# Tiles rounded up to 128 bytes, and root mean square norms rooted by ScalarE from the bank of sums

## The chip, the cores and the metric

The kernel runs on one core of a Trainium2 chip. The metric is the device time of one execution in microseconds (us). A core has five engines that run their own instruction streams and wait for each other by semaphores: PE (TensorE, matmuls; its weight loads are shown as PEld), DVE (VectorE), ACT (ScalarE), POOL (GpSimd) and SP (SyncE, which here issues the weight transfers). Matmuls write banks of PSUM, [128, 512] float32 each; everything else lives in SBUF, 128 partitions wide.

## What is computed

Two transformer-like blocks in a row over 512 tokens of width 1024, all float32. Cut to what matters here:

```python
def rms_norm(x, g):
    y = x * lax.rsqrt(jnp.mean(x * x, axis=-1, keepdims=True) + EPS)    # EPS = 1e-6
    return y * g

# first block
h = rms_norm(x, norm1_g) * (1 + sc1) + sh1
proj = h @ w_in + b_in                      # attention, and a convolution of three taps
y = concat([rms_norm(y_attn, ..), rms_norm(y_conv, ..)])
x = x + g1 * (y @ w_o)
h = rms_norm(x, norm2_g) * (1 + sc2) + sh2
u = h @ w_up                                # gate, val: 2 x 2816 columns
f = silu(causal_dwconv3(gate, w, b)) * val
x = x + g2 * (f @ w_down)
x = rms_norm(x, final_norm_g)
# second block, two layers: rwkv time mix, then a gated spatial unit, each with
# x = x + rms_norm(mixer(rms_norm(x)));  x = x + rms_norm(swiglu(rms_norm(x)))
```

The time mix shifts the tokens by one, `xx = shift(h) - h`, and projects `h + xx * mix` by three matrices of 1024 x 1024.

## The kernel before

Activations are kept transposed: a tile has 128 channels as partitions and the 512 tokens as its row, so x is [128, 8, 512]. The program is one straight line per engine (with loops over pairs of units inside the feed-forward stages), written out by hand, and the stages follow each other: setup, first mixer, first feed-forward stage (`ffn0`, with the convolution), both norms between the blocks, time mix (shift, 24 projection units, eight rounds of the block recurrence, output projection `out_tm`), second feed-forward stage (`ffn1`), gate stage (16 units, then output projection `out_gu`), third feed-forward stage (`ffn2`), output.

**Weight units.** Every large product goes by units of weights. SP loads a unit into `raw` (four slots), ACT copies its upper half as float32r into `whi` (line 226), DVE subtracts for the lower half `wlo` (line 232), and PE does three matmuls for each k tile (lines 247 to 249):

```python
pe.matmul(dst, hi, rhs_hi(k), start=first and k == 0, stop=False)
pe.matmul(dst, hi, rhs_lo(k), start=False, stop=False)
mm = pe.matmul(dst, lo, rhs_hi(k), start=False, stop=last and k == kts - 1)
```

A unit of eight k tiles is 24 matmuls of 128 x 128 weights with a moving tile of 512 columns in float32r. The moving tiles are fh_hi and fh_lo in the up parts of the feed-forward stages (44 units each), f_hi and f_lo in the down parts, xs_hi and xs_lo in the three projections of the time mix (24 units), h, ys, gh and us elsewhere. ACT may overwrite a half of `whi` when the unit two before is done; SP may overwrite `raw` when DVE has made the lower half.

**Norms.** There are twelve. ACT squares the tiles, POOL adds the squares (or PE sums tile by tile), and PE sums over the channels with a matrix of ones into bank 4 (`pe_sums`, lines 328 to 340, or `pe_sum_of`). Then DVE makes mean plus epsilon into the tile var (`dve_mean`, lines 344 and 446), ACT takes the root in place (`act_root`, line 326), and DVE the reciprocal (`dve_rstd`, line 351), after which the tile rstd is ready. The next sum into bank 4 waits for the semaphore of the mean (`var_ready`). The norms: norm1 (setup), norm_cv and norm_at (the two halves of the first mixer's output, right behind each other on the same bank), the norm before ffn0 (its tiles wait for rstd), norm_f (line 1573 takes the reciprocal of a second root made from another bank at the same time, `both`), the norms of the four outputs out_tm, ffn1, out_gu, ffn2 (their tiles are added to x only with rstd), and the norms led into ffn1, the gate stage (norm_g) and ffn2, whose rstd is applied only after the first products.

**Where tiles lie.** Tiles are placed one after another in each partition, every one at the next multiple of 32 bytes, and a later stage uses the bytes of an earlier one again. x, raw, whi, wlo, tmp, sq, var, rstd and vecs start at multiples of 128, and the first tile of a stage as well. Then, in bytes past a multiple of 128:

| tile ahead, its bytes | tiles behind it | before |
|---|---|---|
| gbuf [P, 2, 514], 4112 | fh_hi0, fh_lo0, gsq | 32 |
| hb [P, 8, 513], 16416 | xx, xs_hi, xs_lo | 32 |
| invf [P, 1], 4 | pos_i, spread, k_t, v_tok, prj, p_t | 96 |
| st [P, 2, 12], 96 | gb_sb, cbuf | 64 |
| cbuf [P, 2, 514], 4112 | cacc, ada_acc, x_tok, vrow, late | 96 |
| ends 96, nk_sb 32, ng_sb 32 | cent2 | 32 |
| cent2 [P, 64] 256, not_ka 32 | AR, B_t and all tiles of the block rounds | 64 |
| v_st [P, 56], 224 | v_tk, ws_in, wsT, bs_row, bs | 96 |

All other moving tiles of float32r products (h, f, ys, gh, us, and fh of the second and third feed-forward stages) are at 0.

Other lines that the prediction names: 938, 1020, 2542, 2936 (small float32 matmuls on k_t, p_t, cent2 and wsT), 648 (PE's first use of the constants that POOL makes at the start, which waits for 18 of them), 865 and 2072 (ACT from a bank with a bias column), 1510 and 1673 (DVE, lower halves of f and xs).

Of the kernel before, what the change touches and what calls it, by code (L numbers as in the profile page):

```python
# [22 lines left out]
ALU = mybir.AluOpType  # L23
# [14 lines left out]
KA = DA // P  # L38
RAW = 4
EPS = 1e-6  # L40
TWO_PI = 2 * np.pi
# [77 lines left out]
def build(nc, A, out):  # L119
# [25 lines left out]
    gain = sb("gain", [P, KD])  # L145
    cact = sb("cact", [P, KD])
    bank = [ctx.enter_context(nc.psum_tensor(f"bank{i}", [P, T], F32)) for i in range(8)]
    NORM_BANK, ADA_BANKS = 4, (7, 6, 6)
# [125 lines left out]
    class Norm:  # L274
# [4 lines left out]
        def __init__(self, src, n, ready, eps=EPS, rstd_=None, var_=None, slots=None):  # L279
            self.src, self.n, self.ready, self.eps, self.slots = src, n, ready, eps, slots  # L280
            self.rstd = rstd[:, :] if rstd_ is None else rstd_
            self.var = var[:, :] if var_ is None else var_
            self.sq0, self.acc0 = sq_ready.claim(n), acc_step.claim(0 if slots else n - 2)
            self.sum0, self.var0, self.std0, self.rstd0 = (
                c.claim(1) for c in (sum_step, var_ready, std_ready, rstd_ready))

# [37 lines left out]
        def act_root(self, act):  # L324
            act.wait_ge(var_ready.sem, self.var0 + 1)
            act.activation(self.var, self.var, ACT.Sqrt).then_inc(std_ready.sem, 1)

        def pe_sums(self, pe):
            wait(pe, var_ready.sem, self.var0)
            if self.slots is not None:  # L330
                for k in range(self.n):
                    pe.wait_ge(sq_ready.sem, self.sq0 + k + 1)
                    mm = pe.matmul(bank[NORM_BANK][:, :], ones[:, :], self.slots[k], start=k == 0, stop=k == self.n - 1)
                mm.then_inc(sum_step.sem, 1)
                return
            pe.wait_ge(acc_step.sem, self.acc0 + self.n - 2)
            pe.matmul(bank[NORM_BANK][:, :], ones[:, :], sq_sum[:, :], start=True, stop=False)
            pe.wait_ge(sq_ready.sem, self.sq0 + self.n)
            pe.matmul(bank[NORM_BANK][:, :], ones[:, :], sq[:, (self.n - 1) % 2, :], start=False, stop=True)\
              .then_inc(sum_step.sem, 1)  # L340

        def dve_mean(self, dve):
            dve.wait_ge(sum_step.sem, self.sum0 + 1)
            dve.tensor_scalar(self.var, bank[NORM_BANK][:, :], 1.0 / (self.n * P), self.eps,
                              ALU.mult, ALU.add).then_inc(var_ready.sem, 1)

        def dve_rstd(self, dve, mean=True):
            if mean:
                self.dve_mean(dve)
            dve.wait_ge(std_ready.sem, self.std0 + 1)  # L350
            dve.reciprocal(self.rstd, self.var).then_inc(rstd_ready.sem, 1)  # L351
            dve.wait_ge(rstd_ready.sem, self.rstd0 + 1)
# [69 lines left out]
    class LeadNorm(Norm):  # L422
# [3 lines left out]
        def __init__(self, src, n, ready):  # L426
            self.src, self.n, self.ready, self.eps = src, n, ready, EPS
            self.rstd, self.var = rstd[:, :], var[:, :]
            self.sq0, self.summed0 = sq_ready.claim(n), sq_summed.claim(n)
            self.var0, self.std0, self.rstd0 = (c.claim(1) for c in (var_ready, std_ready, rstd_ready))  # L430

# [5 lines left out]
        def pe_sum_of(self, pe, k):  # L437
            if k == 0:
                wait(pe, var_ready.sem, self.var0)
            pe.wait_ge(sq_ready.sem, self.sq0 + k + 1)  # L440
            pe.matmul(bank[NORM_BANK][:, :], ones[:, :], sq[:, k % 2, :], start=k == 0, stop=k == self.n - 1)\  # L441
              .then_inc(sq_summed.sem, 1)

        def dve_mean(self, dve):
            dve.wait_ge(sq_summed.sem, self.summed0 + self.n)
            dve.tensor_scalar(self.var, bank[NORM_BANK][:, :], 1.0 / (self.n * P), self.eps,
                              ALU.mult, ALU.add).then_inc(var_ready.sem, 1)

# [101 lines left out]
    c_row = sbs(mixer1, "c_row", [KD, P])  # L550
    invf = sbs(mixer1, "invf", [P, 1])
    pos_i = sbs(mixer1, "pos_i", [NT, P], I32)
    pos_f = sbs(mixer1, "pos_f", [NT, P])
# [5 lines left out]
    p_t = sbs(mixer1, "p_t", [P, 2, 4 * P])  # L559
    st = sbs(mixer1, "st", [P, 2, 12])  # L560
    gb_sb = sbs(mixer1, "gb_sb", [P, 2, T])
    cbuf = sbs(mixer1, "cbuf", [P, 2, T + 2])
    cacc = sbs(mixer1, "cacc", [P, 2, T])
# [39 lines left out]
    def pool_setup(pool):  # L603
# [31 lines left out]
        for q in range(NT):  # L635
            pool.wait_ge(const_ready, 14 + q)
            pool.affine_select(out=copies, in_=copies, compare_op=ALU.not_equal, fill=1.0, base=-32 * q,
                               pattern=[[0, NT], [-1, 32]], channel_multiplier=1).then_inc(const_ready, 1)

    CONSTS, MORE_CONSTS = 10, 18  # L640

# [496 lines left out]
    def dve_mixer1(dve):  # L1138
        dve_positions(dve)
        for n in range(len(BY_DVE)):  # L1140
            if n == 2:
                dve_angles(dve)
            if n == len(BY_DVE) - 4:
                norm1.dve_mean(dve)
            if n == len(BY_DVE) - 3:
                norm1.dve_rstd(dve, mean=False)
            dve_early(dve, n)
# [23 lines left out]
        norm_cv.dve_rstd(dve)  # L1171
        norm_at.dve_mean(dve)
        split_lo(dve, first[N_IN + 2])
        norm_at.dve_rstd(dve, mean=False)
        ada_add(dve, 1)
# [90 lines left out]
    class FFN:  # L1266
# [3 lines left out]
        def __init__(self, tag, at0, before, gains, shift, w_gate, w_up, w_down, conv, out_gains, final=False):  # L1270
# [7 lines left out]
            if conv:  # L1278
                self.gbuf = sbs(mem, "gbuf", [P, 2, T + 2])
            with ExitStack() as part:  # L1280
# [278 lines left out]
    def dve_both_norms(dve):  # L1559
# [10 lines left out]
           .then_inc(both_step, 1)  # L1570
        norm_f.dve_mean(dve)
        dve.wait_ge(both_std, 1)
# [8 lines left out]
    def dve_final(dve, k):  # L1581
        if k == 0:
            norm_f.dve_rstd(dve, mean=False)
        dve.scalar_tensor_tensor(x[:, k, :], x[:, k, :], v("final", k), rstd[:, :], ALU.mult, ALU.mult)\
# [18 lines left out]
    shift_mem = ExitStack()  # L1603
    hb = sbs(shift_mem, "hb", [P, KD, T + 1])
    xx = sbs(shift_mem, "xx", [P, KD, T])
# [219 lines left out]
    ng_sb = sbs(bm, "ng_sb", [P, 2 * NT])  # L1825
    cent2 = sbs(bm, "cent2", [P, CH])
    not_ka = sbs(bm, "not_ka", [P, KD])
# [613 lines left out]
    def dve_consts(dve):  # L2441
        dve.wait_ge(masks_ready, MASKS)
        dve.tensor_scalar(not_ka[:, :], vecs[:, col["k_a"]:col["k_a"] + KD], -1.0, 1.0, ALU.mult, ALU.add)\
           .then_inc(consts_ready, 1)
        dve.tensor_scalar(cent2[:, :], eye2[:, :], 1.0 / HD, None, ALU.subtract).then_inc(consts_ready, 1)

# [87 lines left out]
    def pe_turn_v(pe, n, j):  # L2534
# [5 lines left out]
        for t in range(NT):  # L2540
            for e in range(2):
                mm = pe.matmul(bank[Y_BANK[e]][:, col64(t)], v_[hr[e], t * P:(t + 1) * P], cent2[hr[e], :],  # L2542
                               start=True, stop=True)
# [327 lines left out]
    us_l = sbs(gu, "us_l", [P, KD, T], F32R)  # L2871
    v_st = sbs(gu, "v_st", [P, 6 * NT + NT * KD])
    v_tk = sbs(gu, "v_tk", [P, NT, D])
    ws_in = sbs(gu, "ws_in", [P, KD, P])
    wsT = sbs(gu, "wsT", [P, KD, P])
    bs_row = sbs(gu, "bs_row", [1, KD * P])
    bs = sbs(gu, "bs", [P, KD, P])
    LN_EPS = 1e-5
    gs_landed, wsT_done, wsT_ready, bs_done, bs_ready = (sem(n) for n in (
# [166 lines left out]
    def dve_gate(dve):  # L3046
# [58 lines left out]
        for n in range(N_GU):  # L3105
# [22 lines left out]
            if n == 0:  # L3128
                norm_g.dve_mean(dve)
                split_lo(dve, at_g(1).plus(2))  # L3130
                norm_g.dve_rstd(dve, mean=False)
            if n < N_GU - 1:
# [153 lines left out]
```

## Time and profile before

| | us |
|---|---|
| median of 3 runs | 2136.16 |
| lowest and highest run | 2132.23, 2136.9 |
| the profiled execution, its own time | 2140.12 |
| its span, first to last instruction | 2138.0 |

| engine | busy us | share of the span |
|---|---|---|
| PE | 1995.3 | 93% |
| DVE | 1080.3 | 51% |
| ACT | 781.2 | 37% |
| POOL | 240.9 | 11% |

The mean granted clock of PE is 0.957 of full. Times in the profile count from the start of the span. A matmul's busy time overlaps the next one's, so the pace of a stream is read from starts, not from durations. In a timeline a bracket at the end of a row is the idle time of the engine before it and who ended it; `x4` means four instructions merged in one row. A float32 matmul (not float32r) is shown as two passes.

### The profile page before, as it was taken

How to read it: one execution, taken by the hardware profiler on the slowest of the kernel's cores; microseconds unless marked ns; L12 is line 12 of the kernel's file. 1: busy time of each engine (PE TensorE's matmuls, PEld its weight loads, DVE VectorE, ACT ScalarE, POOL GpSimd, SP SyncE). 2: the span in 40 equal slices, each digit the busy share in tenths (PEclk: the TensorE clock that was granted, in tenths of full speed). 3: DMA queues.
4: the chain of work that ended last, by engine and by line, in shares of the span. 5: the costliest groups of instructions: out<-in, count | busy, mean ns of one | idle time of the engine just before them, and what ended most of it. 6: DMA issues, size and time to landing. Idle time of an engine off the chain costs nothing.

```text
span 2138.0 us, 35027 instructions
## 1 busy us (share of the span) xinstructions
PE 1995.3 (93%) x14351; PEld 1567.9 (73%) x14351; DVE 1080.3 (51%) x1579; ACT 781.2 (37%) x1237; POOL 240.9 (11%) x269
## 2 busy tenths in 40 slices
PE   6998989999997999899979899999979989999997
PEld 5776768888883677777757588888857858888885
DVE  6776765454325644678642644342265554443223
ACT  4333333333222345567523433322245443333221
POOL 1100000000024000322211011110100001111110
PEclk8999989999998999899988999999999989999998
DMA  9544223333332132000002133333222213333321
GB/s 299 173 123 128 79 68 89 98 88 113 95 90 59 59 90 73 6 10 10 5 26 69 51 97 98 98 113 103 80 57 82 79 53 98 95 98 105 109 81 40
DMA packets 311052, 181.02 MB, mean 85 GB/s; under 512 B 16381, under 2 KB 303763, under 8 KB 310932
## 3 DMA queue, kind: packets, MB, share of 16 engines
q1 hardware_dynamic: 305506, 162.29, 25.8%
q0 software_dynamic: 4608, 16.78, 2.5%
q8 instruction: 92, 1.51, 0.3%
q10 hardware_dynamic: 818, 0.21, 0.0%
q14 instruction: 28, 0.23, 0.0%
HBM read 177.16 MB, written 2.10 MB: 84 GB/s over the span
## 4 chain that ended last, share of the span: by engine, by line
PE 60%; DVE 5%; issue 5%; ACT 2%; POOL 1%; DVEq 0%; ACTq 0%; POOLq 0%
PE bank L247 16%; PE bank L249 15%; PE bank L248 15%; PE bank L1985 4%; PE bank L441 1%; PE bank L1775 1%; PE bank L2482 1%; PE bank L2476 1%; DVE rstd L351 1%; PE bank L2583 1%; POOL gsq L1449 1%; PE bank L2693 0%; PE bank L2542 0%; PE bank L2694 0%; DVE x L1240 0%
## 5 line engine op out<-in xcount | busy, mean ns | idle before, releaser
L232 DVE TENSOR_TENSOR wlo<-raw,whi 128x1024 fp32r<-128x1024 f32 (+1 forms) x262 | 340.6, 1300 | 711.7 <-ACT whi L226 711.7
L226 ACT ACTIVATE whi<-raw 128x1024 fp32r<-128x1024 f32 (+1 forms) x262 | 292.9, 1118 | 744.0 <-PE bank L249 736.6
L247 PE MATMUL bank<-fh_hi,whi 128*128 128x512 f32 x1056 | 420.4, 398 | 24.9 <-DVE fh_lo L415 17.4
L248 PE MATMUL bank<-fh_lo,whi 128*128 128x512 f32 x1056 | 414.7, 393 | 0.0
L249 PE MATMUL bank<-fh_hi,wlo 128*128 128x512 f32 x1056 | 414.7, 393 | 0.0
L247 PEld LDWEIGHTS bank<-fh_hi,whi 128*128 128x128 f32 x1056 | 199.1, 189 | 83.0 <-DVE fh_lo L415 28.3
L248 PEld LDWEIGHTS bank<-fh_lo,whi 128*128 128x128 f32 x1056 | 199.3, 189 | 44.4 <-issue 1.9
L249 PEld LDWEIGHTS bank<-fh_hi,wlo 128*128 128x128 f32 x1056 | 199.1, 189 | 44.2
L247 PE MATMUL bank<-f_hi,whi 128*128 128x512 f32 x528 | 205.4, 389 | 0.0
L248 PE MATMUL bank<-f_lo,whi 128*128 128x512 f32 x528 | 205.4, 389 | 0.0
L249 PE MATMUL bank<-f_hi,wlo 128*128 128x512 f32 x528 | 205.4, 389 | 0.0
L1541 POOL TENSOR_TENSOR sq<-sq,rstd 128x512 f32<-128x512 f32 x44 | 80.1, 1820 | 457.2 <-ACT sq L1404 457.2
L249 PEld LDWEIGHTS bank<-f_hi,wlo 128*128 128x128 f32 x528 | 99.1, 188 | 20.7
L248 PEld LDWEIGHTS bank<-f_lo,whi 128*128 128x128 f32 x528 | 99.1, 188 | 20.6
L247 PEld LDWEIGHTS bank<-f_hi,whi 128*128 128x128 f32 x528 | 99.1, 188 | 20.4
L2026 POOL TENSOR_TENSOR MTb<-MT,m_level 128x256 f32<-128x256 f32 x80 | 65.4, 845 | 340.2 <-DVE MT L2295 283.2
L1406 ACT ACTIVATE f_hi<-tmp 128x512 f32 (+1 forms) x66 | 41.7, 632 | 154.0 <-DVE tmp L1507 154.0
L247 PE MATMUL bank<-xs_hi,whi 128*128 128x512 f32 x192 | 77.3, 403 | 2.9 <-DVE wlo L232 2.9
L248 PE MATMUL bank<-xs_lo,whi 128*128 128x512 f32 x192 | 75.8, 395 | 0.0
L249 PE MATMUL bank<-xs_hi,wlo 128*128 128x512 f32 x192 | 75.8, 395 | 0.0
L1510 DVE TENSOR_TENSOR f_lo<-tmp,f_hi 128x512 f32 (+1 forms) x66 | 45.7, 693 | 59.2 <-ACT f_hi L1406 59.2
L1507 DVE TENSOR_TENSOR tmp<-bank,sq 128x512 f32<-128x512 f32 x66 | 45.5, 689 | 55.1 <-POOL sq L1541 54.6
(418 smaller groups left out, 3097.1 us busy)
## 6 DMA issues: line engine op xcount, KB each, us to landing
raw<-in_w_up_dram SPq DMA_DIRECT2D x44, 512.0 KB, 3.8
raw<-in_ffn_w_gate_dram SPq DMA_DIRECT2D x44, 512.0 KB, 3.8
raw<-in_ffn_w_up_dram SPq DMA_DIRECT2D x44, 512.0 KB, 3.8
raw<-in_ffn_w_down_dram SPq DMA_DIRECT2D x32, 704.0 KB, 4.6
late<-in_ada_w_dram POOLq DMA_DIRECT2D x32, 512.0 KB, 4.2
raw<-in_rwkv_w_rkv_dram SPq DMA_DIRECT2D x24, 512.0 KB, 4.0
raw<-in_w_down_dram SPq DMA_DIRECT2D x16, 704.0 KB, 4.6
early<-in_ada_w_dram SPq DMA_DIRECT2D x16, 512.0 KB, 14.7
```

Source lines behind the costliest of these rows:

```text
L226: act.activation(whi[:, at.slot, 0:kts * P], raw_unit(at, kts), ACT.Copy).then_inc(hi_ready, 1)
L232: dve.tensor_tensor(wlo[:, at.slot, 0:kts * P], raw_unit(at, kts), whi[:, at.slot, 0:kts * P].bitcast(F32), ALU.subtract).then_inc(lo_read ...
L247: pe.matmul(dst, hi, rhs_hi(k), start=first and k == 0, stop=False)
L248: pe.matmul(dst, hi, rhs_lo(k), start=False, stop=False)
L249: mm = pe.matmul(dst, lo, rhs_hi(k), start=False, stop=last and k == kts - 1)
L351: dve.reciprocal(self.rstd, self.var).then_inc(rstd_ready.sem, 1)
L1406: act.activation(tile_at(self.f_hi, p), ft[:, q, :], ACT.Copy).then_inc(fhi_ready.sem, 1)
L1507: dve.tensor_tensor(ft[:, q, :], bank[2 * q + 1][:, :], acc[:, q, :], ALU.mult)\
L1510: dve.tensor_tensor(tile_at(self.f_lo, p), ft[:, q, :], tile_at(self.f_hi, p).bitcast(F32), ALU.subtract).then_inc(f_ready.sem, 1)
L1541: pool.tensor_tensor(sq[:, q, :], sq[:, q, :], rstd[:, :], ALU.mult).then_inc(s_scaled.sem, 1)
L1985: mm = pe.matmul(q[k][0], q[k][1], q[k][2], start=True, stop=True)
L2026: POOLm.done(pool.tensor_tensor(MTb[:, i % 2, e, :, :], MT[:, e, :, :], m_level[:, i + 1:i + 2, :].to_broadcast([P, NT, CH]), ALU.mult), f ...
```

## The change

Tiles of odd size are made larger, or moved behind others, so that all large tiles start at multiples of 128 bytes; a column of epsilon of 128 bytes is added ahead of the staged tiles, filled by one memset of POOL at the start. The DVE mean of every norm is gone: ACT takes the root of the bank itself, with the scale 1/(n P) and the epsilon column as bias, and waits for PE's sum; the next sum into bank 4 waits for the root (`std_ready`). The root of the second quantity in the step `both` stays.

```diff
+PAD = 64
...
+    eps_col = sb("eps_col", [P, 32])
...
         def act_root(self, act):
-            act.wait_ge(var_ready.sem, self.var0 + 1)
-            act.activation(self.var, self.var, ACT.Sqrt).then_inc(std_ready.sem, 1)
+            act.wait_ge(sum_step.sem, self.sum0 + 1)
+            act.activation(self.var, bank[NORM_BANK][:, :], ACT.Sqrt, bias=eps_col[:, 0:1], scale=1.0 / (self.n * P))\
+               .then_inc(std_ready.sem, 1)
 
         def pe_sums(self, pe):
-            wait(pe, var_ready.sem, self.var0)
+            wait(pe, std_ready.sem, self.std0)
...
-        def dve_mean(self, dve):
-            dve.wait_ge(sum_step.sem, self.sum0 + 1)
-            dve.tensor_scalar(self.var, bank[NORM_BANK][:, :], 1.0 / (self.n * P), self.eps,
-                              ALU.mult, ALU.add).then_inc(var_ready.sem, 1)
-
-        def dve_rstd(self, dve, mean=True):
-            if mean:
-                self.dve_mean(dve)
+        def dve_rstd(self, dve):
             dve.wait_ge(std_ready.sem, self.std0 + 1)
...
         def pe_sum_of(self, pe, k):
             if k == 0:
-                wait(pe, var_ready.sem, self.var0)
+                wait(pe, std_ready.sem, self.std0)
...
-    st = sbs(mixer1, "st", [P, 2, 12])
+    st = sbs(mixer1, "st", [P, 2, 52])
...
-    cbuf = sbs(mixer1, "cbuf", [P, 2, T + 2])
+    cbuf = sbs(mixer1, "cbuf", [P, 2, T + PAD])
...
+        pool.memset(eps_col[:, :], EPS).then_inc(const_ready, 1)
+
+    CONSTS, MORE_CONSTS = 10, 19
...
-                self.gbuf = sbs(mem, "gbuf", [P, 2, T + 2])
+                self.gbuf = sbs(mem, "gbuf", [P, 2, T + PAD])
...
-    hb = sbs(shift_mem, "hb", [P, KD, T + 1])
+    hb = sbs(shift_mem, "hb", [P, KD, T + PAD // 4])
...
-    cent2 = sbs(bm, "cent2", [P, CH])
+    cent2 = sbs(bm, "cent2", [P, CH + 16])
```

Not shown: LeadNorm's root and sum get the same change with its own semaphore (`sq_summed`); the calls of `dve_mean` go, in `dve_mixer1` (norm1, norm_at), `dve_both_norms` and `dve_gate`; st is placed right behind invf; cent2 is read by its first 64 columns; v_st is placed behind bs.

## Rows read from the trace of the kernel before

**Rows 1.** The page's first part: busy time, share of the span, instructions.

```profile
PE 1995.3 (93%) x14351; PEld 1567.9 (73%) x14351; DVE 1080.3 (51%) x1579; ACT 781.2 (37%) x1237; POOL 240.9 (11%) x269
```

**Rows 2.** The page's fourth part: the chain that ended last, by line.

```profile
PE bank L247 16%; PE bank L249 15%; PE bank L248 15%; PE bank L1985 4%; PE bank L441 1%; PE bank L1775 1%; PE bank L2482 1%; PE bank L2476 1%; DVE rstd L351 1%; PE bank L2583 1%; POOL gsq L1449 1%; PE bank L2693 0%; PE bank L2542 0%; PE bank L2694 0%; DVE x L1240 0%
```

**Rows 3.** Timeline of PE, first feed-forward stage: start us, us, engine, line, operation.

```profile
350.03 0.39 PE L247 MATMUL bank<-fh_hi,whi 128*128 128x512 f32 x1
...
355.63 0.39 PE L247 MATMUL bank<-fh_hi,whi 128*128 128x512 f32 x1
```

**Rows 4.** Timeline of PE, second feed-forward stage, up part.

```profile
1350.06 0.39 PE L247 MATMUL bank<-fh_hi,whi 128*128 128x512 f32 x1
...
1355.50 0.39 PE L247 MATMUL bank<-fh_hi,whi 128*128 128x512 f32 x1
```

**Rows 5.** Timeline of PE, projections of the time mix; brackets: idle before, releaser.

```profile
727.98 0.40 PE L247 MATMUL bank<-xs_hi,whi 128*128 128x512 f32 x1
...
733.58 0.40 PE L247 MATMUL bank<-xs_hi,whi 128*128 128x512 f32 x1
...
766.92 0.47 PE L247 MATMUL bank<-xs_hi,whi 128*128 128x512 f32 x1 [1.24 <-DVE wlo L232]
```

**Rows 6.** Timeline of PE, first feed-forward stage, down part.

```profile
590.05 0.39 PE L247 MATMUL bank<-f_hi,whi 128*128 128x512 f32 x1
...
595.49 0.39 PE L247 MATMUL bank<-f_hi,whi 128*128 128x512 f32 x1
```

**Rows 7.** Timeline of PE, sums of norm_cv and norm_at.

```profile
222.49 1.88 PE L333 MATMUL bank<-sq,ones 128*128 128x512 f32 x4
...
228.69 1.88 PE L333 MATMUL bank<-cacc,ones 128*128 128x512 f32 x4
```

**Rows 8.** Groups by line and form: busy us, mean ns, idle before, releasers.

```profile
L1510 DVE TENSOR_TENSOR f_lo<-tmp,f_hi 128x512 f32 x54 | 37.4, 693 | 50.8 <-ACT f_hi L1406 50.8
...
L1673 DVE TENSOR_TENSOR xs_lo<-sq,xs_hi 128x512 fp32r<-128x512 f32 x24 | 16.5, 686 | 0.6
```

**Rows 9.** Timeline of all engines, end of the time mix's output projection.

```profile
1178.38 0.69 DVE L344 TENSOR_SCALAR var<-bank 128x512 f32<-128x512 f32 x1 [1.03 <-PE bank L339]
1179.11 0.63 ACT L326 ACTIVATE var<-var 128x512 f32<-128x512 f32 x1 [1.94 <-DVE var L344]
1179.77 3.35 DVE L351 RECIPROCAL rstd<-var 128x512 f32<-128x512 f32 x1 [0.69 <-ACT var L326]
...
1186.23 0.79 PE L247 MATMUL bank<-fh_hi,whi 128*128 128x512 f32 x1 [7.89 <-DVE fh_lo L415]
```

**Rows 10.** Instructions of lines 865 and 2072: ns minimum/median/maximum.

```profile
L865 ACT ACTIVATE prj<-bank,vecs x6: 669/672/673, 58.4 to 86.5; 128x512 f32<-128x512 f32 x6
...
L2072 ACT ACTIVATE tmp<-bank,vecs x8: 679/695/700, 827.2 to 1039.9; 128x512 f32<-128x512 f32 x8
```

**Rows 11.** Timeline, end of the second feed-forward stage.

```profile
1559.09 1.28 ACT L326 ACT_TABLE_LOAD   x1
...
1560.28 0.69 DVE L344 TENSOR_SCALAR var<-bank 128x512 f32<-128x512 f32 x1 [0.86 <-PE bank L339]
```

**Rows 12.** Timeline of ACT after norm1.

```profile
39.63 1.06 ACT L226 ACTIVATE whi<-raw 128x1024 fp32r<-128x1024 f32 x1 [6.25 <-DMA raw<-in_w_in_dram]
```

**Rows 13.** Timeline of PE, first sum of norm_at.

```profile
226.87 1.98 PE L333 MATMUL bank<-gb_sb,ones 128*128 128x512 f32 x4 [0.78 <-DVE var L344]
```

**Rows 14.** Timeline of DVE at norm_f.

```profile
670.87 0.68 DVE L344 TENSOR_SCALAR var<-bank 128x512 f32<-128x512 f32 x1
...
671.64 3.35 DVE L1573 RECIPROCAL rstd<-sq_sum 128x512 f32<-128x512 f32 x1
```

**Rows 15.** Timeline of PE's weight loads, fourth unit of the second feed-forward stage.

```profile
1213.93 0.19 PEld L247 LDWEIGHTS bank<-fh_hi,whi 128*128 128x128 f32 x1 [0.29 <-DVE wlo L232]
```

**Rows 16.** Timeline of PE, first use of POOL's constants.

```profile
9.28 0.55 PE L648 MATMUL bank<-pos_f,quarter 4*128 4x128 f32 x1 [5.36 <-DVE pos_f L678]
```

**Rows 17.** One stretch: length, busy us of PE, PEld, DVE, ACT, POOL, PEclk, DMA, GB/s.

```profile
282.00:291.00 9.00, 1.70 (x3) 0.34 (x2) 6.69 (x6) 2.08 (x3) 0.00 (x0) 0.50 0.00 0
```

More of the change, by code:

```diff
@@ L283, in __init__ @@
             self.sq0, self.acc0 = sq_ready.claim(n), acc_step.claim(0 if slots else n - 2)
-            self.sum0, self.var0, self.std0, self.rstd0 = (
-                c.claim(1) for c in (sum_step, var_ready, std_ready, rstd_ready))
+            self.sum0, self.std0, self.rstd0 = (c.claim(1) for c in (sum_step, std_ready, rstd_ready))
         def act_slot_free(self, act, k):
@@ L429, in __init__ @@
             self.sq0, self.summed0 = sq_ready.claim(n), sq_summed.claim(n)
-            self.var0, self.std0, self.rstd0 = (c.claim(1) for c in (var_ready, std_ready, rstd_ready))
+            self.std0, self.rstd0 = (c.claim(1) for c in (std_ready, rstd_ready))
         def act_square(self, act, k):
@@ L442, in pe_sum_of, with act_root @@
               .then_inc(sq_summed.sem, 1)
[L444 to L447, printed above, removed]
+        def act_root(self, act):
+            act.wait_ge(sq_summed.sem, self.summed0 + self.n)
+            act.activation(self.var, bank[NORM_BANK][:, :], ACT.Sqrt, bias=eps_col[:, 0:1], scale=1.0 / (self.n * P))\
+               .then_inc(std_ready.sem, 1)
     w_in, w_o, ada_w = (A[n].rearrange("a k n -> (a k) n") for n in ("w_in", "w_o", "ada_w"))
@@ L638, in pool_setup @@
                                pattern=[[0, NT], [-1, 32]], channel_multiplier=1).then_inc(const_ready, 1)
-    CONSTS, MORE_CONSTS = 10, 18
+        pool.memset(eps_col[:, :], EPS).then_inc(const_ready, 1)
+    CONSTS, MORE_CONSTS = 10, 19
     def pe_setup(pe):
@@ L1142, in dve_mixer1 @@
                 dve_angles(dve)
-            if n == len(BY_DVE) - 4:
-                norm1.dve_mean(dve)
             if n == len(BY_DVE) - 3:
-                norm1.dve_rstd(dve, mean=False)
+                norm1.dve_rstd(dve)
             dve_early(dve, n)
@@ L1171, in dve_mixer1 @@
         norm_cv.dve_rstd(dve)
-        norm_at.dve_mean(dve)
         split_lo(dve, first[N_IN + 2])
-        norm_at.dve_rstd(dve, mean=False)
+        norm_at.dve_rstd(dve)
         ada_add(dve, 1)
@@ L1570, in dve_both_norms @@
            .then_inc(both_step, 1)
-        norm_f.dve_mean(dve)
         dve.wait_ge(both_std, 1)
@@ L1582, in dve_final @@
         if k == 0:
-            norm_f.dve_rstd(dve, mean=False)
+            norm_f.dve_rstd(dve)
         dve.scalar_tensor_tensor(x[:, k, :], x[:, k, :], v("final", k), rstd[:, :], ALU.mult, ALU.mult)\
@@ L2444, in dve_consts @@
            .then_inc(consts_ready, 1)
-        dve.tensor_scalar(cent2[:, :], eye2[:, :], 1.0 / HD, None, ALU.subtract).then_inc(consts_ready, 1)
+        dve.tensor_scalar(cent2[:, 0:CH], eye2[:, :], 1.0 / HD, None, ALU.subtract).then_inc(consts_ready, 1)
     def dve_first(dve, o):
@@ L2541, in pe_turn_v @@
             for e in range(2):
-                mm = pe.matmul(bank[Y_BANK[e]][:, col64(t)], v_[hr[e], t * P:(t + 1) * P], cent2[hr[e], :],
+                mm = pe.matmul(bank[Y_BANK[e]][:, col64(t)], v_[hr[e], t * P:(t + 1) * P], cent2[hr[e], 0:CH],
                                start=True, stop=True)
@@ L2871, in build @@
     us_l = sbs(gu, "us_l", [P, KD, T], F32R)
-    v_st = sbs(gu, "v_st", [P, 6 * NT + NT * KD])
     v_tk = sbs(gu, "v_tk", [P, NT, D])
@@ L2877, in build @@
     bs = sbs(gu, "bs", [P, KD, P])
+    v_st = sbs(gu, "v_st", [P, 6 * NT + NT * KD])
     LN_EPS = 1e-5
@@ L3128, in dve_gate @@
             if n == 0:
-                norm_g.dve_mean(dve)
                 split_lo(dve, at_g(1).plus(2))
-                norm_g.dve_rstd(dve, mean=False)
+                norm_g.dve_rstd(dve)
             if n < N_GU - 1:
```

## The prediction

> **What bounds the kernel now.** I read the page first. PE is busy for 93% of the span and DVE for 51% [rows 1], and the chain that ended last consists for 46% of the span of the three matmuls of a weight unit, lines 247 to 249 [rows 2]. So two things count: how fast a stream of these matmuls runs, and how long PE stands still between streams. For the first I asked for the timeline of PE alone inside long streams, where no row has idle time before it, and took the time from one unit (24 matmuls) to the next. For the second I read the timeline of all engines wherever PE stands still.
>
> **The pace of a stream.** In the up part of the first feed-forward stage line 247 comes round after 24 matmuls from 350.03 to 355.63: 5.60 us, 233.3 ns each [rows 3]. In the second feed-forward stage, same lines and shapes, it takes from 1350.06 to 1355.50: 5.44 us, 226.7 ns [rows 4]. The projections of the time mix go from 727.98 to 733.58, again 5.60 us [rows 5]; the down part of the first feed-forward stage, which reads the aligned f_hi and f_lo, from 590.05 to 595.49, 5.44 us [rows 6]. The two slow streams are the two whose moving tiles (fh_hi0 and fh_lo0, xs_hi and xs_lo) start 32 bytes past a multiple of 128; those of all fast ones start at a multiple. The odd-sized gbuf and hb ahead of them cause it, and the change rounds both up. That is 0.16 us per unit.
>
> Not every read of such a tile is dearer. The plain float32 sums over cacc, 96 bytes past a multiple of 128, take 1.88 us for four passes, and so do those over the aligned sq [rows 7]. DVE writes xs_lo in 686 ns and the aligned f_lo in 693 [rows 8]. So I count the alignment of everything else (behind st, cbuf, ends and v_st) at nothing: it is read as float32 or by the other engines. The bounds are nothing and 6.7 ns for each of the 368 passes of the 184 small float32 matmuls of lines 938, 1020, 2542 and 2936, 2.5 us. A loss is excluded by rows 4 and 6, where all tiles are aligned and the pace is the best there is.
>
> The Trainium skill speaks against this term: its page "SBUF — State Buffer", section "Specifications (TRN2)", gives cachelines of 16 bytes, and by them a start 32 bytes off is as good as any, so that the padding would bring nothing. The measured 233.3 against 226.7 ns disagree, and I go by them.
>
> **The change part by part.**
>
> *First feed-forward stage.* 44 units run on fh; at 0.16 us they save 7.0 us if PE stays the bound. The second stage does like work beside it and runs at 226.7 ns [rows 4], so it should. The first products of the first two units are paced by DVE: I take 0.1 off. **6.9 us**, bounds 6.0 and 7.1.
>
> *Time mix.* 24 units on xs: 3.84 us. In each of the second and third projections PE works off 39 matmuls of its first units and then waits for DVE (766.92, idle 1.24) [rows 5]. That wait hangs on the end of the unit before, so what PE gains in these 39 it only waits longer: 0.26 us, twice. The first two units of the first projection lie between low-rank products; I count half of their 0.32. **3.2 us**, bounds 2.5 and 3.8.
>
> *Norms, the exposed ends.* After the time mix's output projection DVE makes the mean from PE's sums at 1178.38 (0.69), ACT roots it at 1179.11 (0.63), DVE inverts it from 1179.77, and PE restarts at 1186.23 after 7.89 of idle time [rows 9]. From the mean's start to the reciprocal's start is 1.39 us. Changed, ACT starts where the mean did, reads a bank and has a column as bias; the rows nearest to that, a bank and a bias column on ACT, have medians of 672 and 695 ns, 700 at most [rows 10]. I take 0.68 and 0.03 for the hand-over, 0.71 in place of 1.39: **0.68** saved, bounds 0.66 and 0.69. The norm before the first feed-forward stage has the same form: 0.68.
>
> The Trainium skill, "ScalarE: Activation LUTs", section "What ACT_TABLE_LOAD costs", gives 280 ns plus 0.833 ns per element with a bias pointer, an estimate of 0.71 us for 512 elements; by it all ends together would save 0.15 us less.
>
> At three other ends ACT first loads its table, from 1559.09 for 1.28, until 1560.37, while the mean starts at 1560.28 [rows 11]. The mean hid this; the root waits some 0.1 for it. These three (second feed-forward stage, gate stage, third feed-forward stage) save 0.57 each. Five exposed ends: 3.08.
>
> *Norms, the covered ones.* norm1: its root waits for a table load, but after it ACT waits 6.25 us for w_in, until 39.63 [rows 12]: nothing; without that cover the longer root costs 0.05. norm_cv: PE's sums for norm_at wait for the mean today (226.87) and for the root tomorrow, since the bank is free only then [rows 13]: 0.69 against 0.68, nothing for PE. DVE comes 0.67 earlier to its reciprocal, which takes 0.3 off PE's wait for the first squares after it. norm_f: the reciprocal waits for another root and starts at 671.64; DVE's mean runs beside that root and ends at 671.55 [rows 14]: nothing. The norms led in with the second and third feed-forward stage: DVE makes the fourth weight unit's lower half after the reciprocal, and PE's weight side stands 0.29 for it [rows 15]: 0.15 each. norm_g: PE has four banks of slack, nothing. Together 0.6, bounds 0 and 1.3. **All norms 3.7 us**, bounds 2.7 and 4.4.
>
> *The rest.* POOL gets one more memset ahead of PE's first constants. PE starts on them at 9.28, released by DVE's cast of the positions and not by POOL [rows 16]: nothing; uncovered 0.1. No DMA is added or moved, SP and POOL are passed by nothing, and DVE's queue loses twelve means. ACT's root now waits for PE in place of DVE; it waits shorter, and behind it stand a weight copy (line 226) and the table for what follows, which SP's loads and DVE's lower halves wait for: they come earlier too.
>
> **The sum.** 6.9 + 3.2 + 3.7 = 13.8 us. The profiled execution took 2140.12 us (span 2138.0) and is 4.0 above the median of the runs, 2136.16. It would become 2126.3, and the median 2122.4.
>
> **Rivals.** A: the pace is a matter of the stage, not of the start address. Then only the norms count: 2132.5. For it: both slow streams have partners of their own (a convolution, a mix) on DVE and ACT. Against it: these differ, and yet both streams have the same pace to 0.1 ns, and the first stage changes its pace where its tile changes [rows 3, 5, 6]. 6%. The skill's cachelines, above, would lead here.
>
> B: the padding works and the norms give nothing, because ACT's read of the bank starts late or takes 1.3 us: 2126.1. Against it: ACT's other reads of banks [rows 10]. 8%.
>
> C, the slower side: PE's clock. It is granted at 0.50, the lower level of 1.2 GHz, from 282 to 291 [rows 17], while PE has little to do before the first feed-forward stage and where it starts again. Every later standstill now comes at another moment, and a low stretch may reach further into a stream, where each us of it costs 0.5 us. To undo 13.8 us and lose 4.3 more takes 36 us more of low clock inside streams, six at each of six standstills. It decides from there on: about 2141. 2%.
>
> D: part of the 6.7 ns stays, from something that rounding to 128 does not remove. Half of it: 2127.4. 6%.
>
> The forecast itself has 78%.
>
> **The numbers.** A measurement of this kernel can tell about 0.2%, 4.3 us, from no change. The predicted time is that of the forecast, 2122.4. Its bounds are 11.2 (6.0 + 2.5 + 2.7) and 15.3 (7.1 + 3.8 + 4.4), or 17.8 with the small float32 matmuls, and the runs shown lie between 2132.23 and 2136.9; that makes 2117 to 2125.5. Reaching to B and D it becomes 2117 to 2128.5. Faster by over 0.2%: the forecast, B, D and what scatter adds from A: 0.93. Within: the rest of A, 0.05. Slower: C, 0.02.
>
> **What would show it.** In the changed profile the streams on fh in the first feed-forward stage and on xs come round in 5.44 us per unit; 5.60 in both is A, 5.52 is D. DVE has no mean; ACT's roots from the bank take 0.67 to 0.70; from the end of PE's last sum to the reciprocal pass some 0.75 us, and PE's idle time before the second feed-forward stage is 7.2. Roots of over 1.3 us are B. Low clock stretches that reach far into streams are C. The block stage between the time mix and its output projection keeps its length; if it shrinks, the small float32 matmuls were dearer than rows 7 say.

## The result, and the profile after

The changed kernel takes 2158.43 us (median of 4 runs, 2155.94 to 2163.84) against 2136.53 for the kernel before in the same comparison: a ratio of 1.0104, 95% interval 1.0090 to 1.0119, 22 us slower. The forecast was 2122.4, 14 us faster, in a range of 2117.0 to 2128.5. Size and sign are wrong. Of all executions behind this document one, the sixth of e8_eps_before_weights, ran at a mean granted clock of 0.822 and took 2302.86 us; no median or ratio here holds it.

The page of the changed kernel, its first part and the chain by line (the three matmuls of a unit are now lines 249 to 251):

```profile
PE 2021.0 (94%) x14351; PEld 1570.4 (73%) x14351; DVE 1072.4 (50%) x1567; ACT 781.8 (36%) x1237; POOL 242.8 (11%) x270
...
PE bank L249 16%; PE bank L250 16%; PE bank L251 16%; PE bank L1977 4%; PE bank L436 1%; PE bank L2474 1%; PE bank L1767 1%; PE bank L2468 1%; DVE rstd L346 1%; PE bank L2575 1%; POOL gsq L1442 1%; PE bank L2534 0%; PE bank L2685 0%; PE bank L2686 0%; PE bank L2660 0%
```

Against [rows 1, 2] DVE lost 12 instructions and 7.9 us, as it should, while PE gained 25.7 us of busy time on exactly as many instructions. The matmuls themselves became slower. Where, the same view as in [rows 3 to 6] tells. Timeline of PE, over 24 matmuls (a unit of eight k tiles; a down part has units of eleven, and the 24 are cut out of them), in this order: up part of the first feed-forward stage, its down part, the time mix, the up and down parts of the second feed-forward stage:

```profile
350.08 0.40 PE L249 MATMUL bank<-fh_hi,whi 128*128 128x512 f32 x1
...
355.65 0.39 PE L249 MATMUL bank<-fh_hi,whi 128*128 128x512 f32 x1
...
589.89 0.39 PE L249 MATMUL bank<-f_hi,whi 128*128 128x512 f32 x1
...
595.46 0.40 PE L249 MATMUL bank<-f_hi,whi 128*128 128x512 f32 x1
...
727.01 0.39 PE L249 MATMUL bank<-xs_hi,whi 128*128 128x512 f32 x1
...
732.61 0.39 PE L249 MATMUL bank<-xs_hi,whi 128*128 128x512 f32 x1
...
1349.80 0.40 PE L249 MATMUL bank<-fh_hi,whi 128*128 128x512 f32 x1
...
1355.40 0.40 PE L249 MATMUL bank<-fh_hi,whi 128*128 128x512 f32 x1
...
1459.71 0.39 PE L249 MATMUL bank<-f_hi,whi 128*128 128x512 f32 x1
...
1465.31 0.39 PE L249 MATMUL bank<-f_hi,whi 128*128 128x512 f32 x1
```

5.57, 5.57, 5.60, 5.60 and 5.60 us. The granted clock is 1.00 from 340 to 360, from 580 to 600 and from 1340 to 1360 us in both kernels, so it is not what differs. The two streams that took 5.60 before hardly moved, and the streams that took 5.44 before, the best pace there was, now take as long. The norms, on the other hand, did what they were meant to do. Timeline of all engines at the end of the time mix's output projection:

```profile
1178.46 0.69 ACT L327 ACTIVATE var<-bank,eps_col 128x512 f32<-128x512 f32 x1 [1.22 <-PE bank L341]
1179.18 3.35 DVE L346 RECIPROCAL rstd<-var 128x512 f32<-128x512 f32 x1 [1.76 <-ACT var L327]
...
1185.64 0.79 PE L249 MATMUL bank<-fh_hi,whi 128*128 128x512 f32 x1 [7.22 <-DVE fh_lo L410]
```

The root from the bank takes 0.69, the reciprocal starts 0.72 after the root does, and PE stood idle for 7.22 in place of 7.89 [rows 9].

Lengths of the stages in us, each from the start of its first matmul to the start of the next stage's, in the profiled executions of three kernels; the third is the changed kernel with one line moved, an experiment below:

| from, to | before | changed | line moved |
|---|---|---|---|
| up part of the first feed-forward stage | 248.4 | 247.7 | 241.7 |
| its down part, to the last matmul | 119.5 | 122.5 | 119.5 |
| projections of the time mix, first xs to last | 165.7 | 165.5 | 163.1 |
| up part, second feed-forward stage | 250.9 | 258.0 | 250.8 |
| its down part, to the last matmul | 119.5 | 123.0 | 119.5 |
| up part, third feed-forward stage | 251.1 | 257.5 | 250.8 |
| its down part, to the last matmul | 119.5 | 123.0 | 119.5 |

### The profile page after: what moved, and what is told of

Read it like the earlier page. It is cut to its first block, busy times and chain, and to the rows that moved or that the text cites. A ratio compares the mean times of both kernels' runs of the same rounds, so it can differ in the third digit from the quotient of the medians.

```text
span 2158.1 us, 35015 instructions
## 1 busy us (share of the span) xinstructions
PE 2021.0 (94%) x14351; PEld 1570.4 (73%) x14351; DVE 1072.4 (50%) x1567; ACT 781.8 (36%) x1237; POOL 242.8 (11%) x270
## 4 chain that ended last, share of the span: by engine, by line
PE 61%; issue 5%; DVE 5%; ACT 2%; POOL 1%; DVEq 0%; ACTq 0%; POOLq 0%
PE bank L249 16%; PE bank L250 16%; PE bank L251 16%; PE bank L1977 4%; PE bank L436 1%; PE bank L2474 1%; PE bank L1767 1%; PE bank L2468 1%; DVE rstd L346 1%; PE bank L2575 1%; POOL gsq L1442 1%; PE bank L2534 0%; PE bank L2685 0%; PE bank L2686 0%; PE bank L2660 0%
## 6 DMA issues: line engine op xcount, KB each, us to landing
early<-in_ada_w_dram SPq DMA_DIRECT2D x16, 512.0 KB, 13.8
```

## The theories

The changed kernel differs from the one before in two ways that I had not told apart: the odd tiles are rounded up, and the new epsilon tile of 128 bytes lies ahead of all staged tiles, so that each of them moves by 128 bytes, also those that were "aligned" and fast. whi and wlo lie ahead of it and stay. No trace records an address: the places are added up from the kernel's own list of tiles, with x, the first, taken to lie at 128 modulo 256, so that whi, 38,912 bytes (152 x 256) further on, and wlo, 11,264 bytes (44 x 256) behind whi, lie at 128 too, in both kernels. Another start of x would shift every place named below alike; the distances between tiles would stay. The fast moving tiles of before are at 128 too, the slow ones at 160, and all of the changed kernel at 0.

**Place**: the pace depends on where the tiles lie. **Program**: it depends on something else that changed, the roots, waits and instruction streams. Four kernels on one chip tell these apart.

## Experiments: half of the change at a time

**e1_norms_only** is the norm change alone. vecs has 114 unused columns, so the epsilon column goes there and no tile moves:

```diff
-    eps_col = sb("eps_col", [P, 32])
...
     vecs = sb("vecs", [P, VB * P])
+    eps_col = vecs[:, 480:512]
...
-                self.gbuf = sbs(mem, "gbuf", [P, 2, T + PAD])
+                self.gbuf = sbs(mem, "gbuf", [P, 2, T + 2])
```

(and st, cbuf, hb, cent2 and v_st as before).

> Only the norm change; every tile lies where it lay in the kernel before, since the epsilon column is the last 32 unused columns of vecs. Theory place (the streams of the changed kernel run at 232 to 233 ns per matmul because the new 128-byte tile moved all staged tiles by 128 bytes): the streams keep the pace of before, 5.60 us per unit on fh of the first feed-forward stage and on xs, 5.44 elsewhere, and the norms save their 3.7 us: about 2132.8. Theory program (the pace changed because the roots, waits and instruction streams changed, not the places): 5.58 to 5.60 per unit everywhere, about 2158.

**e2_padding_only** is the kernel before with the padded and moved tiles, no epsilon tile and the old norms:

```diff
-                self.gbuf = sbs(mem, "gbuf", [P, 2, T + 2])
+                self.gbuf = sbs(mem, "gbuf", [P, 2, T + 64])
...
-    hb = sbs(shift_mem, "hb", [P, KD, T + 1])
+    hb = sbs(shift_mem, "hb", [P, KD, T + 16])
```

(and st, cbuf, cent2 and v_st as in the change).

> Only the odd-sized tiles are padded or moved; no epsilon tile, norms as before. Theory place: all moving tiles start at an odd multiple of 128 (128 past a multiple of 256), where the fast streams of before had them: 5.44 us per unit everywhere, 10.1 us saved, about 2126.4. Theory padding (the new order of tiles itself makes streams slow, for instance by another distance between tiles): 5.58 to 5.60 everywhere, about 2162.

**e3_shift_128** is the kernel before plus one unused tile where the epsilon tile would be:

```diff
     cact = sb("cact", [P, KD])
+    gap = sb("gap", [P, 32])
```

> The kernel before with one unused tile of 128 bytes where the changed kernel has its epsilon column, and nothing else: every staged tile lies 128 bytes further on, the weight tiles stay. Theory place: the streams that ran at 5.44 us per unit now take 5.58 to 5.60; some 1,920 matmuls at 5.7 ns and 3,168 at 6.7 ns more are 32 us, so about 2166 if those on fh of the first stage and on xs (now 32 past a multiple of 256) stay at 5.60. Theory program: nothing changes, about 2136.5.

**e4_eps_in_vecs** is the changed kernel with the epsilon column in vecs:

```diff
-    eps_col = sb("eps_col", [P, 32])
...
+    eps_col = vecs[:, 480:512]
```

> The changed kernel with the epsilon column in the last 32 unused columns of vecs, so that the staged tiles begin where they began before. Theory place: 5.44 us per unit in every stream and the norms' 3.7 us: the forecast comes true, about 2122.7. Theories program and padding: as the changed kernel, about 2158.

Measured, against 2135.39 us for the kernel before:

| | median us | ratio, 95% interval | us per unit: fh first stage, xs, second stage |
|---|---|---|---|
| e1_norms_only | 2131.14 | 0.9987, 0.9972 to 1.0001 | 5.60, 5.60, 5.44 |
| e2_padding_only | 2129.25 | 0.9969, 0.9956 to 0.9982 | 5.44, 5.44, 5.44 |
| e3_shift_128 | 2161.57 | 1.0125, 1.0108 to 1.0142 | 5.62, 5.62, 5.60 |
| e4_eps_in_vecs | 2118.82 | 0.9920, 0.9904 to 0.9937 | 5.44, 5.44, 5.44 |

An unused tile of 128 bytes, alone, costs 26 us. Timeline of PE in e3_shift_128, second feed-forward stage, where the kernel before takes 5.44 [rows 4]:

```profile
1349.61 0.40 PE L248 MATMUL bank<-fh_hi,whi 128*128 128x512 f32 x1
...
1355.21 0.40 PE L248 MATMUL bank<-fh_hi,whi 128*128 128x512 f32 x1
```

Theory program is out, and so is padding as a cause. With the shift taken away, e4_eps_in_vecs gives what was forecast for the whole change: 13.5 to 20.5 us less by its interval, 13.8 forecast. Timeline of PE, first feed-forward stage:

```profile
349.82 0.39 PE L249 MATMUL bank<-fh_hi,whi 128*128 128x512 f32 x1
...
355.26 0.39 PE L249 MATMUL bank<-fh_hi,whi 128*128 128x512 f32 x1
```

What is it about these 128 bytes?

## Experiments: which place is the right one

Either a moving tile is fast at 128 modulo 256 whatever the rest does (**absolute**), or it has to lie where the weights lie (**relative**). All fast streams so far satisfy both.

All kernels of this part start from e4_eps_in_vecs. **e5_offsets** gives each stream a place of its own by unused tiles ahead of it (G_HI is 64, 224 and 160 bytes in the three feed-forward stages):

```diff
+                if G_HI:
+                    sbs(part, f"ghi{tag}", [P, G_HI // 4])
                 h_hi = sbs(part, f"fh_hi{tag}", [P, KD, T], F32R)
...
+    sbs(shift_mem, "gxs", [P, 24])
     xs_hi = sbs(shift_mem, "xs_hi", [P, KD, T], F32R)
...
+    sbs(tm, "gys", [P, 48])
     ys_hi = sbs(tm, "ys_hi", [P, KD, T], F32R)
```

(8 floats ahead of gh_hi, 56 ahead of us_h). **e6_hi_or_lo** moves only one half of a moving tile (in the first stage both gaps are 128, which brings the lower half back to its place):

```diff
+                if G_LO:
+                    sbs(part, f"glo{tag}", [P, G_LO // 4])
                 h_lo = sbs(part, f"fh_lo{tag}", [P, KD, T], F32R)
...
+    sbs(shift_mem, "gxl", [P, 32])
     xs_lo = sbs(shift_mem, "xs_lo", [P, KD, T], F32R)
```

**e7_weights_shift** moves the weights:

```diff
+    sb("gap_w", [P, 32])
     whi = sb("whi", [P, 2, HALF * P], F32R)
     wlo = sb("wlo", [P, 2, HALF * P], F32R)
     ident = sb("ident", [P, P])
     ones = sb("ones", [P, P])
+    sb("gap_a", [P, 96])
```

(and 128 bytes ahead of fh_hi1 and of us_h).

> The kernel of e4_eps_in_vecs with unused tiles ahead of the moving tiles of six streams, so that each stream starts at a place of its own modulo 256: gh at 160, fh of the first stage at 192, xs at 224, fh of the third at 32, ys at 64, fh of the second at 96; us moves by 256 and is again at 128. The weight tiles stay at 128. Theory multiple of 256 (only the place modulo 256 counts, and only 128 is fast): us keeps 5.44 us per unit, all six others take 5.57 to 5.62 (gh 5.60 and fh of the third 5.62, as those places gave before). Theory multiple of 512 (the fast place is 384 modulo 512): us slows down to 5.58 as well. Theory 64 (starts that are no multiple of 64 are slow by themselves, 0 modulo 256 for another reason): the streams at 192 and 64 run at 5.44, those at 160, 224, 32 and 96 slowly.

> The kernel of e4_eps_in_vecs with only one of the two halves of a moving tile at a slow place: in the first feed-forward stage the upper half is at 0 modulo 256 and the lower at 128, in the second and for xs the upper at 128 and the lower at 0, in the third the lower at 160; gh is at 192, us at 0 (256 modulo 512). Of the three matmuls of a k tile two read the upper half and one the lower. Theory own place (each matmul pays for the place of its own moving tile): 5.53 us per unit in the first stage (two thirds of 0.14), 5.49 in the second, third and on xs. Theory pattern (the stream as a whole falls into a beat as soon as one read in three is late): 5.57 to 5.62 in all of them.

> The kernel of e4_eps_in_vecs with both weight tiles 128 bytes further on (at 0 modulo 256) and all staged tiles 512 bytes further on (at 128 modulo 256 as before), except fh of the second stage and us, which are at 0. Theory absolute (the place of the moving tile alone counts): fh of the first and third stage, xs, f, h, ys, gh run at 5.44 us per unit, fh of the second stage and us at 5.57 to 5.60. Theory relative (the moving tile has to lie at the same place modulo 256 as the weights): the other way round, fh of the second stage and us at 5.44 and everything else at 5.57 to 5.60.

Each of the three ran once (2140.07, 2137.73 and 2159.70 us, and 2144.93 for the kernel before), so only the paces of their streams are read. e7_weights_shift decides. Timeline of PE, first feed-forward stage (tiles at 128, weights at 0), then second (both at 0):

```profile
349.93 0.40 PE L251 MATMUL bank<-fh_hi,whi 128*128 128x512 f32 x1
...
355.52 0.40 PE L251 MATMUL bank<-fh_hi,whi 128*128 128x512 f32 x1
...
1350.22 0.39 PE L251 MATMUL bank<-fh_hi,whi 128*128 128x512 f32 x1
...
1355.66 0.39 PE L251 MATMUL bank<-fh_hi,whi 128*128 128x512 f32 x1
```

5.59 and 5.44: 128 is now slow and 0 is fast. us, also at 0, takes 5.44, and every other stream 5.57 to 5.60. **The moving tile has to lie at the same place modulo 256 as the weights.** Two kernels test this rule from other sides.

**e8_eps_before_weights** is the changed kernel with one line moved, all staged tiles at 0:

```diff
+    eps_col = sb("eps_col", [P, 32])
     whi = sb("whi", [P, 2, HALF * P], F32R)
...
     cact = sb("cact", [P, KD])
-    eps_col = sb("eps_col", [P, 32])
```

> The changed kernel with one line moved: the epsilon tile of 128 bytes is placed ahead of the weight tiles and no longer behind them. All staged tiles lie exactly where the changed kernel has them (0 modulo 256), and the weight tiles are now at 0 modulo 256 too. Theory relative (a moving tile has to lie at the same place modulo 256 as the weight tiles): 5.44 us per unit in every stream, about 2119, some 0.8% under the kernel before. Theory absolute (0 modulo 256 is a slow place for a moving tile): 5.57 to 5.60, about 2158.

Measured 2122.54 (median of five) against 2137.73 us; ratio 0.9927, interval 0.9909 to 0.9945, by that ratio 15.6 us faster than before and, by the two ratios (0.9927 over 1.0104), 1.8% faster than the changed kernel. Timeline of PE, the same two stages:

```profile
349.85 0.39 PE L249 MATMUL bank<-fh_hi,whi 128*128 128x512 f32 x1
...
355.29 0.39 PE L249 MATMUL bank<-fh_hi,whi 128*128 128x512 f32 x1
...
1350.10 0.39 PE L249 MATMUL bank<-fh_hi,whi 128*128 128x512 f32 x1
...
1355.54 0.39 PE L249 MATMUL bank<-fh_hi,whi 128*128 128x512 f32 x1
```

5.44 in every stream. This and e4_eps_in_vecs beat both kernels.

**e9_weights_at_160** leaves the tiles unpadded and brings the weights to the two tiles that were slow before:

```diff
+    sb("gap_w", [P, 8])
     whi = sb("whi", [P, 2, HALF * P], F32R)
...
     ones = sb("ones", [P, P])
+    sb("gap_a", [P, 56])
```

> The kernel of e1_norms_only (tiles as in the kernel before, unpadded) with both weight tiles 32 bytes further on, at 160 modulo 256, and all staged tiles 256 bytes further on: fh of the first feed-forward stage and xs are at 160 like the weights, all other moving tiles at 128. Theory relative: the two streams that are slow in the kernel before are the only fast ones, 5.44 us per unit, and all others take about 5.60 (their distance is 224 modulo 256, which gave 5.60 in e5_offsets). Theory start (a start that is no multiple of 64 or 128 costs by itself): fh of the first stage and xs stay at 5.60 or more.

Timeline of PE: first feed-forward stage, up part (160, like the weights) and down part (128); time mix (160); second stage (128):

```profile
349.65 0.39 PE L251 MATMUL bank<-fh_hi,whi 128*128 128x512 f32 x1
...
355.09 0.39 PE L251 MATMUL bank<-fh_hi,whi 128*128 128x512 f32 x1
...
590.01 0.40 PE L251 MATMUL bank<-f_hi,whi 128*128 128x512 f32 x1
...
595.61 0.40 PE L251 MATMUL bank<-f_hi,whi 128*128 128x512 f32 x1
...
726.90 0.39 PE L251 MATMUL bank<-xs_hi,whi 128*128 128x512 f32 x1
...
732.34 0.39 PE L251 MATMUL bank<-xs_hi,whi 128*128 128x512 f32 x1
...
1349.73 0.40 PE L251 MATMUL bank<-fh_hi,whi 128*128 128x512 f32 x1
...
1355.33 0.40 PE L251 MATMUL bank<-fh_hi,whi 128*128 128x512 f32 x1
```

5.44, 5.60, 5.44, 5.60: fast and slow have changed places (one run, 2150.25 us against 2137.73). A tile that starts 32 bytes past a multiple of 128 is as fast as any, if the weights do too.

e5_offsets adds the size of the loss by distance (moving tile less weights, modulo 256). Only us, 256 bytes further on, kept 5.44. Of the expectation that all six others take at least 5.57, one missed: a distance of 64 costs a third of the others. Timeline of PE in e5_offsets, first feed-forward stage (192, the weights at 128):

```profile
350.03 0.39 PE L249 MATMUL bank<-fh_hi,whi 128*128 128x512 f32 x1
...
355.52 0.39 PE L249 MATMUL bank<-fh_hi,whi 128*128 128x512 f32 x1
```

From this run and the others, steady parts of streams:

| distance | us per unit | ns per matmul | seen in |
|---|---|---|---|
| 0 | 5.44 | 226.7 | e4, e8; e7 and e9 where weights and tile moved together |
| 32 | 5.60 | 233.3 | before (fh first stage, xs), e5 (gh) |
| 64 | 5.49 | 228.9 | e5 (fh first stage), e6 (gh) |
| 96 | 5.60 | 233.3 | e5 (xs) |
| 128 | 5.57 or 5.60 | 232.3 or 233.3 | changed, e3, e6 (us), e7 |
| 160 | 5.62 | 234.2 | e3 (fh first stage, xs), e5 (fh third stage) |
| 192 | 5.60 | 233.3 | e5 (ys) |
| 224 | 5.60 | 233.3 | e5 (fh second stage), e9 |

## What stays open: mixed places

e6_hi_or_lo and a last kernel ask which pair of reads must match. **e10_wlo_shift** moves wlo alone by 128, with the halves of fh at chosen places by gaps as in e6_hi_or_lo:

```diff
+    sb("gap_w", [P, 32])
     wlo = sb("wlo", [P, 2, HALF * P], F32R)
```

> The kernel of e4_eps_in_vecs with only wlo moved by 128, so that whi is at 128 and wlo at 0 modulo 256; h, f, xs, ys, gh and us are at 128, fh of the first stage at 0, fh of the second at 128 (upper half) and 0 (lower half), fh of the third the other way round. Theory own weights (each matmul pays if its moving tile is not at the place of its own weights): with everything at 128 one matmul in three is out of place and a unit takes 5.49 to 5.60, none of the streams is fast. Theory next weights (a matmul pays if its moving tile is not at the place of the weights that are loaded while it runs: whi during the first and third of a k tile, wlo during the second): fh of the second stage is in place in all three and runs at 5.44, all others more slowly.

Neither theory of either kernel explains both. Timeline of PE in e6_hi_or_lo, first feed-forward stage (upper half displaced) and second (lower half displaced):

```profile
349.98 0.39 PE L249 MATMUL bank<-fh_hi,whi 128*128 128x512 f32 x1
...
355.47 0.39 PE L249 MATMUL bank<-fh_hi,whi 128*128 128x512 f32 x1
...
1349.71 0.40 PE L249 MATMUL bank<-fh_hi,whi 128*128 128x512 f32 x1
...
1355.31 0.40 PE L249 MATMUL bank<-fh_hi,whi 128*128 128x512 f32 x1
```

5.49 and 5.60: own place had 5.53 and 5.49, pattern at least 5.57 in both. e10_wlo_shift (one run, 2152.29 us against 2137.73) has no fast stream and 5.55 where all moving tiles are at 128, as own weights had it; next weights missed. With A for the place of whi and B for 128 bytes off it, us per unit:

| upper, lower half of the tile | wlo at A (e6) | wlo at B (e10) |
|---|---|---|
| A, A | 5.44 | 5.55 |
| B, A | 5.49 | 5.49 |
| A, B | 5.60 (xs first 5.55) | 5.55 |
| B, B | 5.57 or 5.60 (changed) | 5.60 |

Moving the upper half, which two matmuls of three read, costs less than moving the lower half, which one reads: it is no sum over the matmuls. That speaks against own weights as well: with wlo at A, the row B, A has two matmuls out of place and takes 5.49, the row A, B one and takes 5.60. A lower half displaced by 32 alone (e6, third stage) also takes 5.60. Nor is the match of a moving tile with the weights that are loaded while it streams enough, which A, B with wlo at B has and which takes 5.55. Which reads meet, and by what mechanism, is not settled by these runs. Only this is: all four at one place modulo 256 is fast, and every other combination tried is slower.

## Why the prediction was wrong

**Step that failed: "a loss is excluded by rows 4 and 6, where all tiles are aligned and the pace is the best there is".** In those rows the tiles are at a multiple of 128, but at an odd one, and so are the weights. No stream of before has its tile at an even multiple, and my table of places counted modulo 128, where the shift by the epsilon tile is invisible. I read "32 past a multiple of 128" as the cause; it was "32 away from the weights". Two places had been seen, fast and slow, and any rule that told them apart would have fitted. The rows could not decide, so the range had to hold the other rules. In place of "a loss is excluded", the runs showed a loss of 0.13 to 0.16 us per unit in every stream that had been fast, 25.9 us together.

**First feed-forward stage, 6.9, and time mix, 3.2.** The sizes were right for a layout that the change did not have: with tiles and weights at one place the up part goes from 248.4 to 241.7 and the projections from 165.7 to 163.1 us, 6.7 and 2.6. As built they gave 0.6 and 0.2. PE's stops in the second and third projections, after 12 and after 48 matmuls of each (the forecast counted 39), did grow as forecast: in that kernel by 0.27 and 0.28 us, forecast 0.26.

**The term that was missing.** All other streams lost, but for h in the first mixer, whose stretch lasts 224 to 229 us in the kernels whatever its place and can't be read for this: 7.1 and 6.5 us in the up parts of the second and third stage, 3.5, 3.5 and 3.0 in the three down parts, and 0.6, 0.8 and 0.9 on ys, gh and us, 25.9 together. gh lost less than its 384 matmuls at 5.7 ns (2.2) would, since that stage has waits of its own. Less 0.9 and 3.0 for the norms' exposed ends that is 22.0; the two profiled spans are 20.1 apart and the medians 21.9.

**Norms.** Exposed ends: idle time of PE shorter by 0.67 twice and by 0.57 three times, 3.04 together in place of 3.08 (the forecast's own terms make 3.07). As forecast, the three ends behind a table load gain less. Timeline of ACT and DVE at the first of them (here [rows 11] had the mean in between):

```profile
1569.11 1.28 ACT L327 ACT_TABLE_LOAD   x1
...
1570.40 0.69 ACT L327 ACTIVATE var<-bank,eps_col 128x512 f32<-128x512 f32 x1
1571.12 3.35 DVE L346 RECIPROCAL rstd<-var 128x512 f32<-128x512 f32 x1 [1.68 <-ACT var L327]
```

The 0.6 for the covered norms is below what these runs can tell; e1_norms_only as a whole gives 2.8 us (-0.2 to 6.0), which doesn't tell the norms' 3.7 from nothing; the idle times do.

**The range.** Its upper bound before B and D, 2125.5, is 2125.7 by the numbers named beside it (2136.9 less 11.2), and the 17.8 for the small float32 matmuls didn't enter the lower one. Neither matters against a miss of 30 us above its upper end.

**Rivals.** A (the start address is not the cause) fell, but had the right complaint, that two slow streams don't prove a rule. B fell: the root takes 0.69. C's sign came true without its mechanism: the mean granted clock is 0.958 after 0.957. D had half of the 6.7 ns staying in two streams; 5.6 to 6.7 ns came to all streams that can be read. No rival let the change slow down a stream that was fast, though the text on the change says that the new tile lies ahead of the staged ones.

**The pages.** The prediction set the Trainium skill's cachelines of 16 bytes ("SBUF — State Buffer", section "Specifications (TRN2)") aside because of 233.3 against 226.7 ns. That weighed them wrongly: in e9_weights_at_160 a start 32 bytes off is as good as any, 5.44 us per unit, once the weights have it too. What the forecast drew from them, that the padding brings nothing, still fails: e2_padding_only brings both streams from 5.60 to 5.44. The Trainium skill, "TensorE: Matmul & The Clock Gate", section "Step-by-step: what each phase is for", says that PE has two independent read ports of SBUF and that loading the next weights takes no read bandwidth from the running matmul. By that rule the distance between the two tiles could not matter; here it is worth up to 7.5 ns of 227 per matmul, and the measurement decides.

## What to carry to other kernels

A small tile put ahead of big ones changes the place of all of them: when a change adds or resizes a tile, list where every matmul operand starts, modulo 256 and beside the weights, and not only the tile that was meant. Where a stream of float32r matmuls of 512 columns runs at 233 ns each, look whether its moving tiles and both weight tiles share a place modulo 256; here one moved line was worth 1.8%. And where only two values of a quantity have been seen, one fast and one slow, an untried value belongs in the range as a rival, on both sides.

## What the runs showed of the hardware

- The records show the loss in the matmuls, not in the weight loads. Timeline of PE, then of its weight loads, in the changed kernel's second feed-forward stage:

```profile
1350.27 0.40 PE L251 MATMUL bank<-fh_hi,wlo 128*128 128x512 f32 x1
1350.51 0.39 PE L249 MATMUL bank<-fh_hi,whi 128*128 128x512 f32 x1
1350.74 0.40 PE L250 MATMUL bank<-fh_lo,whi 128*128 128x512 f32 x1
```

```profile
1350.27 0.19 PEld L249 LDWEIGHTS bank<-fh_hi,whi 128*128 128x128 f32 x1
1350.51 0.19 PEld L250 LDWEIGHTS bank<-fh_lo,whi 128*128 128x128 f32 x1
1350.74 0.19 PEld L251 LDWEIGHTS bank<-fh_hi,wlo 128*128 128x128 f32 x1
```

  The matmuls take 0.39 and 0.40 in turn in place of 0.39 [rows 4]; the loads stay at 0.19 [rows 15]. Each load starts with a matmul, so the two read SBUF at the same time.

- At a distance of 128 the same places give two paces, 5.57 and 5.60, and a stream mostly keeps the one it fell into until PE has to wait. In e3_shift_128 the second feed-forward stage runs at 5.60 and the third, with the same tiles, at 5.57. In the changed kernel's time mix the first projection runs at 5.60, the second at 5.58 after a wait of 1.24 us on DVE (from 769.47 to 775.05), and the third at 5.60 again after the next. What chooses was not tried.
- Plain float32 matmuls did not show it in the few passes there are: the sums over cacc, at 96 modulo 256, and over sq, at 128 like its weights ones, take the same 1.88 [rows 7].
- Scatter of some 8 us between kernels sits in the block stage: it took 269.9 us in e1_norms_only and 277.8 in e2_padding_only. Two windows of 50 us at the same place of the stage, 150 us from its start, in the kernel before and in e1_norms_only (columns as in [rows 17]):

```profile
1002.00:1052.00 50.00, 46.00 (x1264) 35.77 (x1266) 36.07 (x82) 31.56 (x68) 12.67 (x16) 0.90 0.03 8
```

```profile
997.60:1047.60 50.00, 47.00 (x1468) 37.46 (x1466) 37.81 (x89) 35.38 (x78) 15.21 (x19) 1.00 0.03 9
```

The granted clock of the first is lower, and PE gets through 1264 matmuls in place of 1468. PE was busy for 92 and 94% of these windows, so idleness of the kind before a feed-forward stage does not explain the dip, and what does was not tried. Differences of a few us between single profiled executions say nothing here; the paces of streams, equal to 0.01 us from unit to unit, do.
